# Attention units in pairs on TensorE: scores side by side, values side by side, a block of gate products between

## What is computed

```python
logits = einsum('bqgrd,bkgd->bgrqk', qb, kb) * scale + bias      # kinds A (window 128), S, W (causal), C (compressed keys)
probs  = softmax(where(valid, logits, NEG))                      # A: with a sink column
out    = einsum('bgrqk,bkgd->bqgrd', probs, vb)
...
y_b    = gates[0] * o_c + gates[1] * o_s + gates[2] * o_w
merged = sigmoid(g_a) * (y_a @ w_up_a) + sigmoid(g_b) * (y_b @ w_up_b)
x      = x + merged @ w_out
```

## Time and profile before

| | |
|---|---|
| median of 3 runs | 2162.04 us (2160.81 to 2163.81) |
| the profiled execution | 2160.59 us, its span 2158.8 us |
| mean granted clock of TensorE | 0.998 |
| busy: PE, PEld, DVE, ACT, POOL | 2128.8, 1724.0, 1192.6, 1001.5, 974.5 us |
| attention, first scores to last values | 1495.8 to 1697.1 us from the span's start |
| gate tiles | 384 matmuls, of which 8 ahead of the first scores |

### The profile page before, as it was taken

The page is one execution under the profiler, slowest core; times in us unless marked ns, Lnnn a source line. Parts: engine busy times, 40 slices in busy tenths (PEclk is TensorE's granted clock), DMA queues, the critical chain, the costliest instruction groups (busy, mean ns, idle before and its releaser), DMA issues.

```text
span 2158.8 us, 28487 instructions
## 1 busy us (share of the span) xinstructions
PE 2128.8 (99%) x10298; PEld 1724.0 (80%) x10298; DVE 1192.6 (55%) x1706; ACT 1001.5 (46%) x1431; POOL 974.5 (45%) x421
## 2 busy tenths in 40 slices
PE   8999999999999999999999999999999899999998
PEld 6788888888887787778888888887766688888886
DVE  7876666321477788877422211422888745666422
ACT  6225544433555565654544434444555654444432
POOL 4444544456543433334544456565121243444563
PEclk9999999999999999999999999999999999999999
DMA  8763566723344433423333223354221132333232
GB/s 349 259 214 127 204 241 251 209 81 100 92 140 151 160 119 137 156 69 98 98 96 94 87 81 97 89 173 138 72 71 40 49 107 78 97 97 97 81 100 72
DMA packets 74481, 273.84 MB, mean 127 GB/s; under 512 B 8648, under 2 KB 11592, under 8 KB 67994
## 3 DMA queue, kind: packets, MB, share of 16 engines
q1 hardware_dynamic: 71018, 266.77, 38.2%
q10 hardware_dynamic: 3376, 5.90, 0.9%
HBM read 269.24 MB, written 8.12 MB: 128 GB/s over the span
## 4 chain that ended last, share of the span: by engine, by line
PE 76%; issue 13%; POOL 5%; DVE 4%; ACT 1%; DMA 1%; SPq 0%; POOLq 0%; ACTq 0%; DVEq 0%
PE bank L586 62%; POOL wlo L535 5%; PE bank L1036 4%; PE bank L1128 2%; PE bank L609 1%; PE bank L1057 1%; PE bank L1093 1%; PE bank L1076 1%; DMA ada_first<-ada_d 1%; PE bank L613 1%; DVE x L1719 1%; DVE ada_first L1745 1%; PE bank L977 1%; PE bank L731 0%; DVE sq L1715 0%
## 5 line engine op out<-in xcount | busy, mean ns | idle before, releaser
L535 POOL TENSOR_TENSOR wlo<-raw,whi 128x1024 fp32r<-128x1024 f32 x382 | 929.2, 2440 | 1112.7 <-ACT whi L1166 1112.6
L1166 ACT ACTIVATE whi<-raw 128x1024 fp32r<-128x1024 f32 x382 | 400.6, 1055 | 537.7 <-PE bank L586 529.2
L586 PE MATMUL bank<-h_hi,whi 128*128 128x512 f32 x1608 | 630.8, 392 | 0.2 <-POOL wlo L535 0.2
L586 PE MATMUL bank<-h_hi,wlo 128*128 128x512 f32 x1608 | 626.3, 389 | 0.0
L586 PE MATMUL bank<-h_lo,whi 128*128 128x512 f32 x1608 | 625.7, 389 | 0.0
L586 PEld LDWEIGHTS bank<-h_hi,whi 128*128 128x128 f32 x1608 | 301.8, 188 | 67.1 <-issue 4.6
L586 PEld LDWEIGHTS bank<-h_hi,wlo 128*128 128x128 f32 x1608 | 301.8, 188 | 63.0
L586 PEld LDWEIGHTS bank<-h_lo,whi 128*128 128x128 f32 x1608 | 301.9, 188 | 62.0
L586 PE MATMUL bank<-g_hi,whi 128*128 128x512 f32 x592 | 230.3, 389 | 0.0
L586 PE MATMUL bank<-g_lo,whi 128*128 128x512 f32 x592 | 230.3, 389 | 0.0
L586 PE MATMUL bank<-g_hi,wlo 128*128 128x512 f32 x592 | 230.3, 389 | 0.0
(11 more groups left out here) (355 smaller groups left out, 2924.6 us busy)
## 6 DMA issues: line engine op xcount, KB each, us to landing
raw<-f_in_d SPq DMA_DIRECT2D x88, 512.0 KB, 3.6
raw<-m_d SPq DMA_DIRECT2D x65, 512.0 KB, 3.7
ada_f<-ada_d SPq DMA_DIRECT2D x24, 1024.0 KB, 6.6
raw<-g_in_d SPq DMA_DIRECT2D x44, 512.0 KB, 3.6
raw<-w_in_d SPq DMA_DIRECT2D x41, 512.0 KB, 3.7
csb<-cs_d SPq DMA_DIRECT2D x32, 640.0 KB, 6.5
ada_a<-ada_d SPq DMA_DIRECT2D x16, 1024.0 KB, 5.0
raw<-a_in_d SPq DMA_DIRECT2D x24, 512.0 KB, 6.2
```

What stands on the lines that cost most here:

```text
L535: nc.gpsimd.tensor_tensor(wlo[:, s], raw[:, s], whi[:, s].bitcast(F32), ALU.subtract).then_inc(lo_ready, 1)
L586: mm = nc.tensor.matmul(psum[bank][:], w[:, s, kk, :], xs[part == "lo"][:, k, :], start=first and kk == 0 and i == 0, stop=last and kk == ...
L1166: nc.scalar.activation(whi[:, s], raw[:, s], ACT.Copy).then_inc(hi_ready, 1)
```

## The change

TensorE takes units two by two. In the step of an even n: scores of n+2, scores of n+3, transposes of n, twelve gate matmuls, transposes of n+1, values of n-1, values of n. Where values of n-1 end one kind or one r (`SEAMS`, n = 4, 26, 30), they go ahead of the gate block. Three gate tiles (`EARLY`) are done as ordinary tiles ahead of attention, into the four rotating banks, and VectorE copies them from there; the fourth takes the place of the first around the first score blocks, and the other twelve (from `ALONE` on) take two pairs each, up to n = 46. In n = 50 the first half of the first `up` tile stands between the transposes. VectorE's gate copies and ScalarE's splits come every fourth unit; low parts of heads 0 and 1 are one to a unit. The sigmoids wait for one gate tile at a time. The softmax passes are as they were.

```diff
-             f_in1=44, f_out1=8, w_in=17, up=16, w_out=8, g_in=44, g_out=8)
+             f_in1=44, f_out1=8, w_in=20, up=16, w_out=8, g_in=44, g_out=8)
...
+EARLY = 3
+ALONE = EARLY + 1
+BLOCK = 12
 LAST_A, LAST_B = NT - 1, PER - 1
...
+SEAMS = [n for n in range(2, NU, 2) if n % PER in (0, LAST_A + 1)]
...
-                    if j:
-                        pe.wait_ge(ga_out, j)
+                    if j > EARLY:
+                        pe.wait_ge(ga_out, j - EARLY)
...
-            for n in range(NU):
-                if n + 2 < NU:
-                    scores(n + 2)
-                j, first = gate_part(n)
-                if 0 < j < GATES:
-                    gate(j, first, first + 8)
-                turn_probs(n)
-                if n >= 1:
-                    values(n - 1)
-            values(NU - 1)
...
+            def gates_early(j):
+                single("w_in", GATE0 + j, wait=False, c=w_chunk(GATE0 + j))
+
+            gates_early(0)
+            fold_parts(1)
+            gates_early(1)
+            compressed(1)
+            gates_early(2)
+            pe.wait_ge(v_out, 4)
+            gate(EARLY, 0, 8)
...
+            scores(0)
+            scores(1)
+            gate(EARLY, 8, 24)
+            for n in range(0, NU, 2):
+                for m in (n + 2, n + 3):
+                    if m < NU:
+                        scores(m)
+                turn_probs(n)
+                if n in SEAMS:
+                    values(n - 1)
+                if n < NU - 4:
+                    gate(ALONE + n // 4, BLOCK * (n // 2 % 2), BLOCK * (n // 2 % 2 + 1))
+                elif n == NU - 2:
+                    pe.wait_ge(scored, NU)
+                    up(0, 0)
+                turn_probs(n + 1)
+                if n and n not in SEAMS:
+                    values(n - 1)
+                values(n)
+            values(NU - 1)
+            for u, half in ((1, 0), (0, 1), (1, 1)):
                 up(u, half)
...
-                if n >= 3 and (n - 3) % PER in (LAST_A, LAST_B):
+                last = n >= 3 and (n - 3) % PER in (LAST_A, LAST_B)
+                if last and n - 2 not in SEAMS:
                     attended(n - 3)
                 if n >= 2:
                     turned_out(n - 2)
-                if n >= 3 and n % 3 == 0 and n // 3 <= GATES:
-                    split_hi(C0["w_in"] + w_chunk(GATE0 + n // 3 - 1) + RING)
+                if last and n - 2 in SEAMS:
+                    attended(n - 3)
+                if n == 1:
+                    split_hi(C0["w_in"] + w_chunk(GATE0 + EARLY) + RING)
+                j = ALONE + (n - 5) // 4
+                if n % 4 == 1 and ALONE <= j < GATES:
+                    split_hi(C0["w_in"] + w_chunk(GATE0 + j) + RING)
                 if n >= NU - 3:
-                    for k in ((0, 1), (2, 3), (4, 5), (6,), ())[n - (NU - 3)]:
+                    for k in ((0, 1), (2, 3), (4,), (5,), (6,))[n - (NU - 3)]:
                         head_split(k)
...
-            act.wait_ge(ga_out, GATES)
             for u in range(8):
                 for i in range(2):
+                    act.wait_ge(ga_out, max(1, 8 * i + u - EARLY + 1))
...
+            for j in range(EARLY):
+                b = (T0["w_in"] + GATE0 + j) % 4
+                done(C0["w_in"] + w_chunk(GATE0 + j))
+                nc.vector.tensor_copy(ga[:, j, :], psum[b][:]).then_inc(bank_free[b], 1)
...
             for n in range(NU + 1):
                 if n < NU:
                     score(n)
                     maximum(n)
-                if n % 3 == 2 and 0 < n // 3 < GATES:
-                    gate_copy(n // 3)
                 if n >= 1:
                     normalised(n - 1)
                 if n == 1:
-                    gate_copy(0)
-                if n == NU - 1:
-                    for k in range(2):
-                        lo_part(h_lo[:, k, :], qk[:, k, :], h_hi[:, k, :], I0["up"] + k)
+                    gate_copy(EARLY)
+                j = ALONE + (n - 5) // 4
+                if n % 4 == 1 and ALONE <= j < GATES:
+                    gate_copy(j)
+                if NU - 2 <= n < NU:
+                    low_head(n - (NU - 2))
             for k in range(2, 7):
-                lo_part(h_lo[:, k, :], qk[:, k, :], h_hi[:, k, :], I0["up"] + k)
+                low_head(k)
```

More of the change, by code:

```diff
@@ L110 @@
 GATES = 16
+EARLY = 3
+ALONE = EARLY + 1
+BLOCK = 12
 LAST_A, LAST_B = NT - 1, PER - 1
-def gate_part(step):
-    j = (step + 2) // 3
-    return j, 8 * ((step + 2) % 3)
+SEAMS = [n for n in range(2, NU, 2) if n % PER in (0, LAST_A + 1)]
 def span(kind, qt):
@@ L1131, in up @@
                     mm.then_inc(chunk_done, 1)
-            for u, half in ((0, 0), (1, 0), (0, 1), (1, 1)):
+            def gates_early(j):
[7 more added lines that the diff above has]
+            gate(EARLY, 0, 8)
+            for b in range(4):
+                pe.wait_ge(bank_free[b], (T0["up"] - 1 - b) // 4 + 1)
+            scores(0)
[19 more added lines that the diff above has]
+            for u, half in ((1, 0), (0, 1), (1, 1)):
                 up(u, half)
@@ L1473, in load_tbias @@
                 load_bias(r, tbias, tbias_in, 8, WB, TB)
-            for u in range(GATE0):
+            for u in range(GATE0 + EARLY):
                 c, b = C0["w_in"] + w_chunk(u), (T0["w_in"] + u) % 4
@@ L1483, in _ @@
                     nc.scalar.activation(stage(3)[0:24, :], psum[b][0:24, :], ACT.Sigmoid).then_inc(bank_free[b], 1)
-                else:
+                elif u < GATE0:
                     nc.scalar.activation(stage(u - QKV["va"]), psum[b][:], ACT.Copy).then_inc(bank_free[b], 1)
@@ L1527, in _ @@
                     split_hi(c + 1 + RING)
-                if u in (13, 16):
+                if u in (13, 17):
                     kv = u // 16
@@ L2160, in gate_copy, with low_head @@
                 nc.vector.tensor_copy(ga[:, j, :], psum[7][:]).then_inc(ga_out, 1)
+            def low_head(k):
+                lo_part(h_lo[:, k, :], qk[:, k, :], h_hi[:, k, :], I0["up"] + k)
             for n in range(NU + 1):
```

## The result

The changed kernel takes 2169.32 us (median of 7 runs, 2168.63 to 2171.47) against 2162.04 us (7 runs) of the kernel before: ratio 1.0033, 95% interval 1.0022 to 1.0044. It is slower by 7.3 us, where 2.5 us less were forecast. The sign was wrong. The time lies inside the range, which was wide (23 us), near its end, on the side of rival (b).

What follows compares the result with a forecast made beforehand. TensorE, busy 99% of the span, was taken as the bound. -13.6 (shapes) - 8.4 (old waits) + 20 (new waits) and some tenths of clock gave -2.5 us: 2159.5 us from 2162.04, range 2148 to 2171.

Steps and rivals of the forecast that it cites:

- rival (b): Transposes n+1: ScalarE's turned copy becomes the bound in every pair; waits 30 to 36 us, 2170 to 2176 us; chance 0.20.
- The shapes: Attention on TensorE: pairing units means fewer changes of array shape, saving 13.6 us (bounds 11 and 15).
- The gate tiles: Three tiles, 16.65 us, move ahead of attention: nothing gained or lost on TensorE, but cover for the softmax is gone.
- part 3: The waits in attention, said to decide: 8.4 us start to start before the change, 20 us after it.
- The waits at the gate blocks: Transposes n+1 wait for ScalarE's copy: 12.9 with splits, 3.3 without, 0.5 at the start; 16.7 us, taken as 15.5.
- the clock: Attention's tail: some tenths of the 1.2 us that the lower clock costs there would be won back.
- the waits before: TensorE's waits in the old order: 6.6 us by busy time, 8.4 us start to start.
- 43 to 22: Whole kernel: chance 0.43 of faster by over 0.2%, 0.22 of slower; 0.35 within 0.2%.
- (a): Attention: the cover suffices, waits stay at 8 to 12 us, time 2148 to 2152 us; chance 0.32.
- (c): Array shapes: the terms are not saved, a drain moves into each block of a pair; 2166 to 2172 us; chance 0.03.
- The signs: Right if, in attention, TensorE idles near 20 us, ended by ScalarE's turned copy, with VectorE busy over 90%.
- GpSimd and the negation: GpSimd's split holds VectorE's negation until it ends; if engines only slowed each other, some 9 us faster than forecast.

Runs made afterwards that it cites:

- e6: Changed kernel with units one by one again, gate blocks of six matmuls, three gate tiles still ahead of attention, no up product in the loop: 2168.86 us.
- e2: Changed kernel with no gate tile ahead of attention; the three return as blocks of 24 in six pairs that waited: 2159.65 us.
- e1: Changed kernel with ScalarE's turned copy of even units put ahead of the exponentials: 2159.89 us.
- e11: e8 with its 16 low-part splits of attention cut to about 0.1 us each, low parts left out: 2144.12 us.
- e4: Changed kernel with 13 low-part splits in attention cut to about 0.1 us each, low parts left out: 2152.72 us.
- e9: As e2, but the six blocks of 24 stand in pairs where the changed kernel waited little: 2164.58 us.
- e8: e3 with ScalarE's last split of the stage moved from behind unit 49 to behind the last turned copy: 2148.83 us.
- e5: Kernel before the change with its 16 low-part splits in attention cut to about 0.1 us each, low parts left out: 2156.26 us.
- e3: Changed kernel with the edits of e1 and e2 together: 2151.27 us.
- e10: e8 with ScalarE's turned copy ahead of the exponentials for odd units too: 2147.88 us.

## Why the prediction was wrong, point by point

**The shapes.** Forecast 13.6 (11 to 15), measured 12.4. The terms read from differences of block lengths were right, within the stated bounds; the missing 1.2 us I cannot place.

**The gate tiles.** "Nothing on TensorE, but cover is gone" was right as a sentence, and its price lies in the waits of part 3, which were worked without these tiles. So it did not spoil the sum. But it was charged to the pairing, and never weighed as a change of its own: by e6 the move costs 7 us even one by one, and without it (e2) the pairing is not slower.

**The waits at the gate blocks.** Forecast 16.7 us in front of transposes behind gate blocks, of which I "took 15.5". From start to start, less the usual distance, they are 16.3. Unit by unit for those that meet a split: forecast 1.0, 1.8, 1.1, 1.1, 0.8, 0.5, 0.7, 0.3, 2.9, 0, 2.7, measured 0.4, 2.0, 1.4, 1.4, 0.8, 0, 0.4, 0.3, 2.3, 1.4, 2.0. This mechanism, its place and its size stood. The discount of 1.2 did not.

**The step that failed.** It is in part 3: the waits were looked for only at transposes of n+1, behind the gate block. Those at transposes of n, ahead of the block, were put at nothing without a reason. But transposes of an even n wait for ScalarE's copy of the odd n-1, which stands in ScalarE's queue behind the exponentials of n+1. The changed kernel waits 4.8 us there (start to start), most of it at transposes 44, 10, 36 and 24. Put into the forecast, these waits alone turn -2.5 into +2.3.

Two more terms were off. First, the clock: 10.2 us at half of the full clock in the stage, during 8.2 of which TensorE worked, so some 4 us, where I had counted on getting back tenths. Rival (b) named it, with one or two us a pause. Second, the waits before: 7.3 us start to start, not 8.4, part of those 8.4 being the slow clock.

The sum with measured terms, from the kernel before to the changed one: -12.4 (shapes) - 7.3 (old waits) + 25.5 (new: 16.3 at gate blocks, 4.8 ahead of them, 4.4 in the tail) + 4.1 - 1.7 (clock) = +8.2, against 8.7 between the two spans. Forecast was -13.6 - 8.4 + 20 - 0.5. Four terms missed on the same side by 1.2, 1.1, 5.5 and 2.9 us. The 5.5 of the new waits, of which 4.8 are those ahead of the blocks, turns the sign by itself; so would the clock's 2.9, just; the first two would not. A sum of terms of 10 to 25 us with a result of 2.5 carries no sign, and the chances should have said so more clearly than 43 to 22.

**The rivals.** (a), that the cover suffices, is refuted by the waits themselves, 22.2 us in the list where it had 8 to 12; its "TensorE's 163.5" does not come out of the rows either, which give 194.7 - 16.65 + 2.8 - 13.6 = 167.2 us of work (measured busy time: 174.0). (b) decides from 22 us of waits on, 0.75 us a pair; there were 25.5 and 4 of clock. Its mechanism, the copy behind the exponentials, is what e1 confirms; its price of 30 to 36 us was too high. (c) is refuted by e11.

**The signs.** TensorE's idle time is 22.6 us, near the 20 named, and ended by ScalarE's copy. VectorE, named at over 90% busy, is at 161.7 of 196.6 us, 82%. So that sign was wrong: TensorE waited although VectorE had time left, which points to the order of the work and not to its amount.

**GpSimd and the negation.** The prediction took a negation to be held until the split ends. In the stage of the changed kernel 12 negations overlap a split; each ends 0.02 to 0.03 us after it, and they take 0.46 to 2.38 us by how early they start, while the reduces beside them keep their length. So it is a hold to the end. e4 prices the whole hold, 16.6 us with the clock's part (at half for 3.4 us instead of 10.2). The 9 us in the prediction were the price between a hold and a mere slowing, and no run measures that.

**Still open.** Why tiles in the wrong pairs (e9) bring half of what they bring in the right ones is argued, from VectorE getting ahead, not shown by a run that changes only that. How much of a run's gain is the clock's is taken from the rows, as no run holds the clock alone.

## What to carry to other kernels

When two steps are put side by side to save a switch, what hung loosely between them becomes a chain inside one turn: count, for every wait, the work that lies between its cause and itself in the old order and in the new, and in each engine's own queue look for an instruction that is ready but stands behind one that isn't. Independent filler work is cover; do not move it out of a stage whose second engine is 84% busy, give it to the turns with the longest chain, and then fix the order on the neighbour. Here the paired order lost 7 us as written and won 13 with the three tiles back, ScalarE's copy of even units moved ahead of the exponentials and one split moved by some 10 us (e8).

## What the runs showed of the hardware

A block of another shape of the array costs 0.15 (values) to 0.21 us (scores) beyond its columns, by the differences of block lengths in the earlier trace rows, and twelve microseconds were won by halving the number of changes (e11 against e5). A reduce on VectorE runs at its length of 0.95 us beside a GpSimd subtraction, a tensor_scalar of two elements a partition takes 1.94 us, ending with it (1546.98 against 1546.95), and 0.18 alone (e4). I had not expected the clock to answer to waits of this size. The busy times by stretch of the changed kernel, for its first fall (columns as in the earlier trace rows):

```profile
1650.20:1653.50 3.30, 3.30 (x28) 2.97 (x28) 0.60 (x2) 0.81 (x3) 0.00 (x0) 0.50 0.08 30
```

TensorE is busy throughout, at half of the full clock (1.2 GHz), right after a body wait of 2.1 us, though the waits over the stage are only a tenth of it. The sum of the waits doesn't decide it: with 7 to 9 us of them (e8, e3) the clock stayed full for the whole stage, and in e10, with 5, it fell once, behind a wait of 1.7 us. The length of the last wait doesn't either: e3 has 3.3 us at transposes 49 and keeps the full clock, e1 has as much there and falls, and e1 also falls at 1524.2, at a wait of 0.8:

```profile
1682.31 0.66 PE L1085 MATMUL bank<-kst,sq 128*128 128x128 f32 x4 [3.32 <-DVE sq L2184]
```

```profile
1524.31 1.09 PE L1074 MATMUL bank<-kst,qk 128*128 128x128 f32 x4 [0.81 <-ACT pt L1575]
```

Each of these is one execution, and the mean granted clock varies between executions of one kernel (0.995 to 0.999 in those of the kernel before). What decides a fall stays open.
